# A hybrid Hyena / attention block on one core: the order in which Hyena's spectrum work and the projections of the attention inputs take turns on three engines

## The reference

```python
pl = modulate(rms_norm(xl, g_mix), sh1, sc1) @ w_in          # all projections of the tokens
hy, q, k, v, nq, nk, nv = split(pl)

def hyena_mixer(u, filt2, conv_w, conv_b, skip):
    u = short_conv(u, conv_w, conv_b)                        # three taps
    v, x1, x2 = split(u, 3)
    v = v * x1
    uf, ff = rfft(v, n=2 * L), rfft(filt2, n=2 * L)
    return x2 * (irfft(uf * ff)[:L] + v * skip)

mix = concat([hyena, gqa(q, k, v), natten(nq, nk, nv)]) @ w_out
x = x + gt1 * mix
x = x + gt2 * swiglu(modulate(rms_norm(x, g_ffn), sh2, sc2))
out = rms_norm(x, g_final)
```

## Time and profile before

| | |
|---|---|
| median of 3 runs | 1261.89 us (1261.7 to 1262.73) |
| the profiled execution, its own time | 1262.73 us |
| its span, first to last instruction | 1260.9 us |
| PE busy | 1236.5 us, 98% |
| DVE busy | 912.0 us, 72% |
| ACT busy | 651.5 us, 52% |
| POOL busy | 344.9 us, 27% |
| share of PE in the chain that ended last | 71% |

### The profile page before, as it was taken

One profiled execution on the slowest core, in us unless ns is written; L12 is line 12 of the kernel. 1 busy time (PEld: TensorE's weight loads), 2 busy tenths in 40 slices (PEclk: granted clock), 3 DMA queues, 4 the chain that ended last, 5 costly groups with the idle time before them and its releaser, 6 DMA issues.

```text
span 1260.9 us, 22752 instructions
## 1 busy us (share of the span) xinstructions
PE 1236.5 (98%) x7872; PEld 650.3 (52%) x7872; DVE 912.0 (72%) x1517; ACT 651.5 (52%) x1238; POOL 344.9 (27%) x341
## 2 busy tenths in 40 slices
PE   8999999999999999999999999999999999999997
PEld 1564656556665666664454444444444444444443
DVE  3879998666779999954368866676666665667586
ACT  2532234556779999963145655444444543412324
POOL 0100000114678999840013322233332210000001
PEclk9999999999999999999999999999999999999999
DMA  9728723235200130021130332222223305997953
GB/s 354 275 75 325 255 81 134 68 93 158 64 25 2 34 133 16 18 84 51 50 100 1 93 92 83 78 68 70 75 83 91 91 28 159 358 341 253 365 181 134
DMA packets 108165, 158.91 MB, mean 126 GB/s; under 512 B 8384, under 2 KB 67264, under 8 KB 106816
## 3 DMA queue, kind: packets, MB, share of 16 engines
q1 hardware_dynamic: 108096, 158.00, 36.8%
HBM read 135.95 MB, written 19.93 MB: 124 GB/s over the span
## 4 chain that ended last, share of the span: by engine, by line
PE 71%; DVE 10%; ACT 9%; issue 6%; POOL 2%; DMA 1%; ACTq 0%; SPq 0%; POOLq 0%; DVEq 0%
PE PS L1222 67%; ACT arena L2129 4%; DVE arena L2553 1%; PE PS L1550 1%; PE PS L1487 1%; PE PS L1296 1%; ACT PS L2132 1%; ACT arena L2132 1%; DMA arena<-weight_sum_rows 1%; DVE arena L3187 1%; DMA arena<-in_w_mod 1%; DVE arena L3190 1%; DVE arena L3067 1%; DVE arena L2949 1%; POOL arena L1093 1%
## 5 line engine op out<-in xcount | busy, mean ns | idle before, releaser
L1222 PE MATMUL PS<-arena 128*128 128x512 f16 (+8 forms) x7272 | 1195.1, 325 | 15.6 <-DMA arena<-in_w_mod 4.8
L1222 PEld LDWEIGHTS PS<-arena 128*128 128x128 f16 (+3 forms) x7272 | 599.4, 100 | 584.6 <-issue 43.7
L2949 DVE SCALAR_TENSOR_TENSOR arena<-arena 128x512 f16<-128x512 f32 x148 | 120.7, 822 | 76.6 <-ACT arena L2217 76.6
L2217 ACT ACTIVATE arena<-arena 128x512 f16<-128x512 f32 x140 | 87.6, 629 | 130.4 <-PE PS L1222 130.4
L2841 DVE TENSOR_REDUCE arena<-PS 128x1 f32<-128x512 f32 (+1 forms) x160 | 106.6, 682 | 8.9 <-PE PS L1222 8.9
L2329 ACT ACTIVATE arena<-arena 128x512 f16<-128x512 f32 x77 | 48.1, 629 | 121.9 <-DVE arena L3100 73.5
L2129 ACT ACTIVATE arena<-PS 128x512 f16<-128x512 f32 x140 | 88.2, 630 | 1.2 <-PE PS L1222 0.7
L1189 POOL TENSOR_TENSOR arena<-arena 128x512 f32<-128x512 f32 x20 | 26.7, 1336 | 222.0 <-DMA arena<-in_w_ffn_in 193.8
L1093 POOL TENSOR_TENSOR arena<-arena 128x512 f16<-128x512 f32 x64 | 73.9, 1156 | 9.4 <-ACT arena L2132 8.1
L1216 POOL TENSOR_TENSOR arena<-arena 128x1 f32<-128x1 f32 x8 | 4.7, 597 | 236.1 <-DVE arena L3241 236.1
L2865 DVE TENSOR_TENSOR arena<-PS,arena 128x512 f16<-128x512 f32 x96 | 65.5, 682 | 4.0 <-ACT PS L2132 3.9
(11 more groups left out here) (208 smaller groups left out, 1168.1 us busy)
## 6 DMA issues: line engine op xcount, KB each, us to landing
arena<-in_w_ffn_out SPq DMA_DIRECT2D x121, 256.0 KB, 4.8
arena<-in_w_mod SPq DMA_DIRECT2D x23, 1024.0 KB, 7.3
arena<-in_w_ffn_in SPq DMA_DIRECT2D x88, 256.0 KB, 3.0
arena<-in_w_in SPq DMA_DIRECT2D x9, 1024.0 KB, 5.5
left_operands<-arena SPq DMA_DIRECT2D x33, 256.0 KB, 2.2
arena<-left_operands SPq DMA_DIRECT2D x3, 2816.0 KB, 12.4
arena<-lay_bias SPq DMA_DIRECT2D x12, 512.0 KB, 3.8
arena<-in_x SPq DMA_DIRECT2D x2, 2048.0 KB, 14.3
```

The source lines that it names most:

```text
L1222: return pe.matmul(out, lhsT, rhs, start=start, stop=stop, skip_group_check=True)
L2217: act.activation(aS[n % RING][:, 0], weight_block(p, b), ACT.Copy, scale=WS).then_inc(blk_hi, 1)
L2949: dve.scalar_tensor_tensor(dst[:, 1], src, WS, dst[:, 0], ALU.mult, ALU.subtract).then_inc(blk_lo, 1)
```

## The change

It writes the lists of the three engines in another order. No instruction is added or dropped, and no semaphore is new; on PE one wait (`hy_rdy` at 5) goes, since the wait for 6 now stands ahead of what it guarded.

```diff
@@ PE
             forward(0)
-            pe.wait_ge(hy_rdy, 5)
-            project(0)
             pe.wait_ge(hy_rdy, 6)
             late_columns(2, 3)
+            project(0)
             project(1)
             pe.wait_ge(spec_rdy, 3)
             forward(1)
@@ ACT
             residues(0)
             slot(0)
             slot(1)
             residues(1)
+            spectrum_hi(0)
             for u in range(2, GROUP0[1]):
                 slot(u)
-                if u == 2:
-                    spectrum_hi(0)
@@ DVE
             residue_sums(0)
+            slot(0)
             late_sum(2)
             multiply(0)
-            slot(0)
+            slot(1)
             fold(0)
-            slot(1)
+            slot(2)
             residue_sums(1)
-            slot(2)
-            spectrum_lo(0)
             slot(3)
             multiply(1)
+            spectrum_lo(0)
             slot(4)
             fold(1)
             spectrum_lo(1)
```

## The result

The changed kernel takes 1269.51 us (median of 5, 1266.93 to 1271.88), against 1262.25 us for the one before: ratio 1.0059, 95% interval 1.0045 to 1.0074. I had forecast 1266.2 us, with a range to 1268.2. It is slower, as forecast, but by 7.3 us where I had worked out 4.3. (The forecast stood on the median known then, 1261.89; on 1262.25 the same sum gives 1266.5.) The profiled execution took 1271.47 us, with a span of 1269.7 us: 8.8 us more than the span before.

A forecast was written before the change was run, and what follows sets the result against it. PE bounds the kernel, busy 1236.5 of 1260.9 us, with DVE arriving just in time. First wait 1.60, less 0.32 at turn_qk(0), plus 2.99 at turn_qk(3) gives +4.27 us: 1266.2 us against the median, range 1263.8 to 1268.2.

The forecast's parts named there:

- The first wait, 1.44 us and 0.16 of restart: PE ahead of late_columns(2, 3): waits 1.44 us for hy_rdy at 6, 1.60 with restart (weight loads not made ahead).
- The wait at `turn_qk(0)` goes: PE at turn_qk(0): lo_parts(0) comes early in DVE's new list, saving 0.16 us of wait and 0.16 of restart.
- DVE stands idle for about 3.5 us ahead of `slot(2)`: DVE after fold(0): slot(2) waits for ACT's results with residue_sums(1) queued behind it, losing about 3.5 us.
- PE is held at `turn_qk(3)` until 195.77: PE, there at 192.94, waits 2.83 us for lo_parts(3), 2.99 with restart.
- Where that delay comes from: lo_parts(3) on DVE, 4.19 us later: 1.30 from fold(0) starting later, the rest DVE's idle time and the moved spectrum_lo(0).
- Nothing more behind `slot(4)`: Behind slot(4) the lists are as before, DVE 4.19 us late and PE 4.27; no PE wait at turn_qk(4).
- The sum of the order, +4.27: Whole stretch on PE: 1.60 - 0.32 + 2.99 = +4.27 us.
- The clock stays up: PE's 2.8 us wait: forecast counts no clock loss, since 2.0 us did not suffice; a fall had chance 0.05.
- The price of a fall: If the clock fell at PE's 2.8 us wait, one unit of 5.18 us of matmuls would take twice as long.
- the rival that came true in kind: The clock falls to the 1.2 GHz level where PE stands for 2.8 us: 1271.4 us, chance 0.05.
- Given back later (0.13): PE's gap at 296.40 to 298.40 us fills with the delay: +2.3 us, 1264.2, not slower; chance 0.13.

The follow-up runs named there:

- the kernel with the sums first: DVE's and ACT's edits without PE's, with residue_sums(1) put ahead of slot(2) on DVE; 1265.4 us against 1263.44 for the kernel before, ratio 1.0014.
- the waits filled: Changed kernel with 6 unread matmuls of 512 columns ahead of late_columns(2, 3) and 12 ahead of turn_qk(3); 1266.74 us, ratio 1.0034; repeated, 1266.86, 1.0032.
- the first wait filled: Changed kernel with unread matmuls only in the wait ahead of late_columns(2, 3); 1269.05 us against 1262.68 for the kernel before, ratio 1.0039.
- the kernel with the doubled thin matmuls: Kernel before with late_columns(2, 3) made twice in a row, 3.4 us of one-column matmuls instead of 1.7; 1266.12 us against 1263.44, ratio 1.0021.
- the kernel with the split thin matmuls: Kernel before with 8 more one-column matmuls behind project(1), apart from the first 8; 1262.75 us against 1262.69, ratio 1.0002.
- PE's edit alone: Kernel before with only late_columns(2, 3) and its wait moved ahead of project(0) on PE, DVE and ACT unchanged; 1267.65 us against 1262.68, ratio 1.0034.

## Why the prediction was wrong

- **The first wait, 1.44 us and 0.16 of restart:** right. 1.47 in the trace, released by the instruction named.
- **The wait at `turn_qk(0)` goes:** right.
- **DVE stands idle for about 3.5 us ahead of `slot(2)`:** right, 3.55; and right in its cause. With the cast taken back behind `slot(2)` 1.8 us of it go; the 1.76 that stay are the wait for ACT's own part of `slot(2)`, which the kernel with the sums first fills in part.
- **PE is held at `turn_qk(3)` until 195.77:** right; 195.82 in the execution without a lower clock. The wait was 2.77 for 2.83.
- **Where that delay comes from:** the place was right, one part of my account was not. `spectrum_lo(0)` has no share in it. The delay is 1.30 us by the later start of `fold(0)` and the rest DVE's idle time, less the 0.94 us of the slot that moved ahead of `fold(0)`, which the prediction left out of this account (its chain of starts has it right).
- **Nothing more behind `slot(4)`:** right for the waits. The sum of the order, +4.27, was measured as +4.1 and +4.2 with the waits filled.
- **The clock stays up:** this is the step that failed. I gave the fall 0.05, for the second wait alone, and based that on the gap of 2.0 us in the earlier trace rows, in which the clock stayed at 1.00. In the profiled execution of the changed kernel it falls behind both waits: 4.7 us, which the sum put at nothing, beside the 4.1 of the order. Three things were wrong with the reading. The row shows the gap, and a fall shows behind it: in the kernel with the sums first the window of the gap has 0.99, and the next one 0.51. (The kernel before had none behind it either; the window is below.) The row is one execution, with a gap of 2.05 us: near 300 us the clock falls in two other traces, behind 2.43 us (the first wait filled) and 2.64 us (the sums first), and of 21 executions of the kernel before on one chip 7 took over 1264 us, perhaps for that reason; no trace of such an execution was taken. Length alone does not decide either: the wait of 2.77 us at `turn_qk(3)` was followed by a fall in two traces and not in a third. And thirdly I looked only at how long PE stands still, not at what comes next. The first wait is the shorter one, but it is followed by 1.7 us of matmuls of one column. The rule of the Trainium skill that I quoted (TensorE: Matmul & The Clock Gate, Why this matters for your kernels) speaks of idle gaps. The fall behind the second wait is of its kind, though that wait, 2.77 us, is shorter than the gap that the section names; that a busy PE can lose its clock too is shown by the kernel with the doubled thin matmuls.

The kernel before, behind its gap:

```profile
298.40:302.00 3.60, 3.53 (x41) 2.64 (x42) 2.26 (x8) 3.21 (x9) 1.16 (x1) 1.00 0.65 203
```

The kernel with the sums first, its gap and what follows:

```profile
297.50:299.90 2.40, 0.00 (x0) 0.00 (x0) 0.40 (x1) 1.09 (x4) 0.46 (x1) 0.99 0.25 5
299.90:303.30 3.40, 3.18 (x27) 2.72 (x28) 1.45 (x5) 1.93 (x5) 1.16 (x1) 0.51 0.69 244
```

- **The price of a fall:** I had 5.2 us for one. Measured: 1.38 us for the second fall and 3.3 us for the first, which lasted twice as long; about 1.9 us for the one behind the doubled thin matmuls. I had put a whole unit at half speed; a fall took 3.4 us. So the rival that came true in kind was also priced wrongly, and its 1271.4, near the profiled execution's 1271.47, is luck.
- **Given back later (0.13):** it exists, as the kernel with the split thin matmuls shows, but the gap in the profiled execution of the changed kernel was 1.80 us for 2.05 before. It gave back 0.25 us there. In three traces (the first wait filled, the sums first, the changed kernel on the second chip) the profile names a DVE instruction as what ended it; what sets its length was not tried, and stays open.

No order tried here was faster than the one before. The best, with the sums first, is 0.14% slower. In the earlier trace rows DVE ends `lo_parts` within 0.2 us of the `turn_qk` that waits for it at both ends of the stretch, and PE has no other gap in it, so there seems to be little in the order to win.

## What to carry to other kernels

Where the leading engine's partner arrives just in time, work out each `wait` of a new order from the distances of the old trace: it came out here within 0.1 us. Then ask of every wait put into TensorE not only its length but what PE does right behind it; a wait of 1.5 us next to thin matmuls cost 3.3 us more by the clock in one trace and nothing in two others. Keep transposes of columns and other thin work apart from waits and from each other, and look at several executions, since one trace shows one draw of the clock.

## What was not expected of the hardware

- The clock fell right behind a stretch in which PE was busy throughout with f32 matmuls of one column (3.4 us of them in a row), and not when a block of 24 matmuls of 512 columns stood in their midst (one trace of each).
- The same program on the same chip falls or not from one execution to the next: PE's edit alone gave 1263.34 us at a mean clock of 0.999 and 1269.58 at 0.994.
- Matmuls whose result nobody reads, put into the waits, kept the clock up with the order unchanged: mean clocks of 0.997 to 0.999 in 16 executions, and 1.0034 times the kernel before against 1.0059 without them in the first measurements. On the second chip, 1266.86 against 1268.15 us, the difference is within the noise.
